# Scan preparation of a hybrid decoder step: token mixing all on one engine, key norms in another place

## The reference, cut to what matters

```python
zm = zf + (z_prev - zf) * mu_shift          # token shift, 1696 columns
r, k, v, w_lo, a_lo, g_lo = split(zm)
w_log = -softplus(-(w0 + tanh(w_lo) @ w_decay_up)) - 0.5
decay = exp(-exp(w_log))
a = sigmoid(a0 + a_lo @ w_iclr_up)
g = sigmoid(g_lo) @ w_gate_up
kk = heads(k * k_k)
kk = kk / max(sqrt(sum(kk * kk, -1)), 1e-12)    # per head of 64
k = k * (1.0 + (a - 1.0) * k_a)                 # the "key factor"
y, state = wkv_scan(r, decay, k, v, -kk, kk * a, state)
```

## Time and profile before

| what | value |
|---|---|
| time, median of 3 runs | 1613.26 us (1612.03 to 1622.89) |
| profiled execution: its time | 1620.39 us |
| profiled execution: span | 1618.7 us |
| busy: TensorE, DVE, ACT, POOL | 1256.8, 500.7, 263.7, 211.7 us |
| mean granted clock of TensorE | 0.883 |

### The profile page before, as it was taken

How to read it: one execution, slowest core, us unless ns; L and a number is a source line. 1 busy time by engine, 2 the same in 40 slices (tenths; PEclk the granted TensorE clock), 3 DMA queues, 4 the chain that set the end, 5 groups by cost and what they waited for, 6 DMA issues and landing times. The chain is left out here.

```text
span 1618.7 us, 26083 instructions
## 1 busy us (share of the span) xinstructions
PE 1256.8 (78%) x10498; PEld 775.4 (48%) x10498; DVE 500.7 (31%) x1005; ACT 263.7 (16%) x537; POOL 211.7 (13%) x247
## 2 busy tenths in 40 slices
PE   5999969989994686677455999839878788878881
PEld 3885547679992454333223774513333233323330
DVE  2002357735645452663441211241111101110113
ACT  2000233202220132453000001201111111110110
POOL 0000252100000530243311000001111101110000
PEclk9999989898997697798677999859999999998996
DMA  7022121240001853332726561259999999999964
GB/s 308 17 71 100 43 64 64 80 117 4 5 7 68 248 171 111 100 96 112 220 71 234 203 251 73 109 184 353 404 404 413 407 414 407 406 410 414 413 281 172
DMA packets 89081, 324.86 MB, mean 201 GB/s; under 512 B 25257, under 2 KB 57178, under 8 KB 74282
## 3 DMA queue, kind: packets, MB, share of 16 engines
q1 hardware_dynamic: 69018, 291.80, 46.9%
q0 software_dynamic: 11184, 25.17, 4.8%
q10 hardware_dynamic: 8768, 6.29, 1.3%
HBM read 306.36 MB, written 28.92 MB: 207 GB/s over the span
## 5 line engine op out<-in xcount | busy, mean ns | idle before, releaser
L2489 DVE TENSOR_TENSOR e_g<-e_g,PS 64x512 f32<-64x512 f32 x32 | 22.1, 690 | 332.2 <-ACT e_g L2456 332.2
L289 PE MATMUL PS<-scr,p_w 128*128 128x272 f32 (+2 forms) x448 | 105.2, 398 | 6.1 <-DVE scr L356 6.1
L2402 PE MATMUL PS<-first,e_xs 128*64 128x512 f32 x352 | 89.0, 663 | 22.5 <-DMA first<-in_w_exp_up 21.8
L894 PE MATMUL PS<-scr 128*128 128x272 f32 x384 | 92.6, 404 | 15.2 <-PEq L2559 13.2
L2402 PE MATMUL PS<-second,e_xs 128*64 128x512 f32 x352 | 84.6, 636 | 24.3 <-DMA second<-in_w_exp_up 23.6
L2402 PE MATMUL PS<-e_w,e_xs 128*64 128x512 f32 x320 | 79.7, 655 | 24.7 <-DMA e_w<-in_w_exp_up 24.6
L289 PEld LDWEIGHTS PS<-scr,p_w 128*128 128x128 f32 (+2 forms) x448 | 83.7, 187 | 27.3 <-issue 6.9
L894 PEld LDWEIGHTS PS<-scr 128*128 128x128 f32 x384 | 75.1, 197 | 31.8 <-issue 13.5
L2060 PE MATMUL PS<-m_oT,xe 128*128 128x272 f32 x256 | 64.6, 412 | 22.0 <-DMA m_oT<-scratch_ob_dram 18.2
L2345 POOL DMA_INDIRECT xe<-scratch_h_dram,toks x32 | 30.5, 954 | 386.6 <-PE PS L2392 283.8
L1193 POOL DMA_DIRECT2D c_raw<-in_cmp_pool x48 | 38.1, 796 | 264.3 <-issue 263.4
(11 more groups left out here) (545 smaller groups left out, 2011.1 us busy)
## 6 DMA issues: line engine op xcount, KB each, us to landing
first<-in_w_exp_gate SPq DMA_DIRECT2D x11, 2048.0 KB, 16.6
first<-in_w_exp_up SPq DMA_DIRECT2D x11, 2048.0 KB, 21.0
first<-in_w_exp_down SPq DMA_DIRECT2D x11, 2048.0 KB, 24.0
second<-in_w_exp_gate SPq DMA_DIRECT2D x11, 2048.0 KB, 28.4
second<-in_w_exp_up SPq DMA_DIRECT2D x11, 2048.0 KB, 32.8
second<-in_w_exp_down SPq DMA_DIRECT2D x11, 2048.0 KB, 22.9
e_w<-in_w_exp_gate SPq DMA_DIRECT2D x10, 2048.0 KB, 27.7
e_w<-in_w_exp_up SPq DMA_DIRECT2D x10, 2048.0 KB, 31.9
```

The source lines that it names most:

```text
L289: last = nc.tensor.matmul(out[:, n], w[:, s % NW, c, a:a + m], hT[:, c, n * TH:n * TH + TH], start=(c == 0), stop=(c == KC - 1))
L894: last = M(gate_ps(u)[:, n], wgate[:, u % 2, c, :], hT[:, c, n * TH:n * TH + TH], start=(c == 0), stop=(c == KC - 1))
L2402: last = M(ps, xs[:, b, c, :], w[s][m][:, c * DE:c * DE + DE], start=(c == 0), stop=(c == KC - 1))
L2489: V.tensor_tensor(g[:, b, :], g[:, b, :], psU, ALU.mult).then_inc(h_out, 1)
```

## The change

POOL no longer mixes v. It waits until `mixed` is 2, and only then clears the padding tiles. DVE mixes v as a fourth round, between k and r, with the same instructions as the other rounds; `mixed` rises after chunks 12 and 13 and after r, as before. The semaphore `v_mixed` and the waits on it on DVE and ACT are gone. The key factor's four chunks are split: chunks 0 and 1, then the four multiplications by the inverse norms, then chunks 2 and 3.

```diff
@@ gpsimd
-                pool.wait_ge(par_in, 16)
-                cs = slice(8, 12)
-                shift_rows(G_, link, cs)
-                mu = Pm("mu", 8, 4).unsqueeze(2).to_broadcast([P, 4, T])
-                link(G_.tensor_tensor(v_[:, :, 0:T], v_[:, :, 0:T], mu, ALU.mult))
-                link(G_.tensor_tensor(v_[:, :, 0:T], v_[:, :, 0:T], z[:, cs, 0:T], ALU.add))
-                pool.sem_inc(v_mixed, 1)
+                pool.wait_ge(mixed, 2)
                 link(G_.memset(v_[:, :, T:TP], 0.0))
@@ vector
-                for cs in (slice(12, 14), slice(4, 8), slice(0, 4)):
+                for cs in (slice(12, 14), slice(4, 8), slice(8, 12), slice(0, 4)):
                     shift_rows(V, link, cs)
...
-                    dve.wait_ge(mix_done, {12: 2, 4: 6, 0: 10}[cs.start])
-                    if cs.start != 4:
+                    dve.wait_ge(mix_done, {12: 2, 4: 6, 8: 10, 0: 14}[cs.start])
+                    if cs.start in (12, 0):
                         dve.sem_inc(mixed, 1)
...
-                dve.wait_ge(v_mixed, 1)
                 dve.wait_ge(lora_out, 12)
...
-                for c in range(4):
+
+                def key_factor(c):
                     link(V.tensor_scalar(BK[:, c, 1, 0:T], a_[:, c, 0:T], 1.0, Pm("k_a", c), ALU.subtract, ALU.mult))
                     link(V.scalar_tensor_tensor(out=k_[:, c, 0:T], in0=BK[:, c, 1, 0:T], scalar=1.0, in1=k_[:, c, 0:T],
                                                 op0=ALU.add, op1=ALU.mult))
+
+                for c in (0, 1):
+                    key_factor(c)
                 for c in range(4):
                     dve.wait_ge(norm_mm, c + 1)
                     link(V.tensor_tensor(kk[:, c, 0:T], kk[:, c, 0:T], wide(c % 2), ALU.mult))
                     dve.sem_inc(kk_used, 1)
+                for c in (2, 3):
+                    key_factor(c)
@@ scalar
                 act.wait_ge(mixed, 2)
-                act.wait_ge(v_mixed, 1)
```

More of the change, by code:

```diff
@@ L487, in rwkv @@
         scanned = sem("r_scanned")
-        pchain, v_mixed, mix_done = sem("r_pchain"), sem("r_v_mixed"), sem("r_mix_done")
+        pchain, mix_done = sem("r_pchain"), sem("r_mix_done")
         dchain, achain, s_init = sem("r_dchain"), sem("r_achain"), sem("r_s_init")
```

## The result

| | before | after |
|---|---|---|
| median, 20 runs each | 1617.86 us (1612.03 to 1625.52) | 1612.72 us (1607.50 to 1619.04) |
| ratio, after to before | | 0.9972, 95% interval 0.9959 to 0.9986 |
| profiled execution: time, span | 1620.39, 1618.7 us | 1610.26, 1608.6 us |
| last gate eviction, from the stage's first matmul | 118.49 us | 114.56 us |

The ratio is worth 4.5 us (2.3 to 6.6). The forecast was 8.8. Ratios leave out two executions that were far longer than the rest (1801.43 us with unit 7 between the products, 2059.48 us with 128 partitions and no gap). The last line of the table is the measure used from here on: the start of ScalarE's last gate eviction less the start of the first matmul of the stage `rwkv` (222.19 and 222.13 us).

A forecast was written before the change was run, and what follows sets the result against it. TensorE was taken to bound the changed stretch, 222 to 350 us, through its gaps and slow clock. Part 1's 1.9 plus part 2's 6.9 made 8.8 us, off the median 1613.3 to 1604.5 us; range 1600 to 1613.

The forecast's parts named there:

- Part 1, VectorE's stalls: Mixing of v: 11.3 us of VectorE stalls beside POOL go, closing TensorE's gap before the third gate unit, −1.9 us.
- first signal: `mixed` = 1 comes 3.2 us sooner, ScalarE's tanh starts at 230.3; the second comes 4.6 us sooner, near 250.3.
- Rival 3: Mixing stalls are VectorE's own, not POOL's; the added v round delays TensorE: 2.3 us slower, 1615.6 us; chance 0.03.
- Part 2, the gap: Before norm product 3: multiplications ahead of the second key factor half cut TensorE's idle from 3.96 to 0.7 us.
- Part 2, the hold on POOL: VectorE's multiplications with one PSUM operand and POOL's subtractions do not hold each other; POOL ends 1.2 us sooner.
- Part 2, the clock: Around norm product 3: full clock through the short gap; products 3 and 4 take 2.25 us, unit 7 ends at 296.8.
- stall for unit 8: TensorE waits 0.2 us for gate unit 8's weights, bounds 0 to 1.4 us.
- Rival 1: Clock still falls at the short gap before product 3: 3.8 us come back, gain 5.0 us, 1608.3 us; chance 0.14.
- The shift behind the stage: After the scan starts, barriers make the shift rigid: the last gate eviction's 8.8 us should reappear at the end.
- The absolute time: Whole kernel: 1604.5 us, the median 1613.3 less 8.8 us.
- rival 4: Whole kernel: work shifts, but scatter or a later stage swallows the gain, 1611 to 1614 us; chance 0.13.

The follow-up runs named there:

- unit 7 between the products: Changed kernel with gate unit 7 placed between norm products 2 and 3, key factor chunks 2 and 3 between multiplications 2 and 3; ratio 0.9943 to the kernel before.
- 128 partitions and no gap: Changed kernel with norm products over 128 partitions instead of 8 and only key factor chunk 0 ahead of the multiplications; ratio 0.9952 to the kernel before.
- run with wide products: Changed kernel with norm products over 128 partitions instead of 8, 1.2 us gap kept; ratios 0.9937 and, repeated, 0.9955 to the kernel before.
- two traces without a gap: Changed kernel with only key factor chunk 0 ahead of the multiplications, products over 8 partitions; ratio 0.9954 to the kernel before, last gate eviction at 112.01 and 112.19 us.
- the long gap left in place: Kernel before with only the norm products widened from 8 to 128 partitions, gap 4.16 us; ratio 0.9988, last gate eviction at 117.04 us.

## Why the prediction was wrong

The direction was right and the size was not. By its own steps:

- **Part 1, VectorE's stalls:** right. 3.3 and 8.1 us go; the first signal came at 230.19 (forecast 230.3), the second at 250.0 (250.3), the first gate eviction at 232.93 (233.0), the gap closed for 2.0 us (1.9). Rival 3, that the stalls were VectorE's own, is excluded by the 0.17 and 0.83 us.
- **Part 2, the gap:** 0.99 us where 0.7 were forecast. Relative to TensorE, VectorE's scans start 0.3 us later than in the kernel before.
- **Part 2, the hold on POOL:** right. POOL's subtractions take 1.2 us less, 6.46 and not 7.65, as worked out with no hold from the earlier trace rows; VectorE's first two multiplications take 1.59 us beside them (at 284.64), as long as in the kernel before, where POOL was done (at 289.62). The eviction that releases unit 8's weights follows. In the run with wide products, where unit 7 is fast, the evictions of units 7 and 8 are 297.26 and 304.76, 7.50 apart: a stall of 0.2 us, the forecast's figure. The Trainium skill's rule on the shared SBUF interface (GPSIMD Engine Reference, Specifications), by which VectorE instructions in a 2-port mode or with two SBUF inputs contend with POOL, agrees with these times: a multiplication here has one SBUF and one PSUM input.
- **Part 2, the clock:** this step failed. "Such a gap is shorter than the 1.93 us that left the clock at 1.00, so I count full clock". The comparison took the gap as the only cause. The 1.93 us gap lay between gate units with 128 partitions, the other one in the middle of four products with 8. In the changed kernel the clock fell 0.3 us after the second of these products had ended; in the two traces without a gap it fell while the third ran; with the products over 128 partitions and a gap of 1.2 us it did not fall. Products 3 and 4 took 4.40 us where 2.25 were forecast, and gate unit 7 took 10.06 us where 7.33 were forecast: 2.15 + 2.73 = 4.9 us of the forecast are missing. 8.8 − 4.9 = 3.9, the 3.93 us of the trace, and within the interval of the ratio, 4.5 us (2.3 to 6.6). The 0.2 us by which product 3 came late and the 0.2 us of stall for unit 8, which was not there, cancel.
- **Rival 1** is what happened to the clock, with a chance of 0.14, though not for its reason, the short gap. It was priced at the old slow spell's cost, 3.8 us, and 5.0 us of gain. It was dearer because the spell is as long as before, 10.2 us, but where 2.7 us of the old one fell into idle time, TensorE now works through nearly all of it. Of the 2.97 us taken from the gap, 2.0 had lain in the slow spell; work moved into that time ran at half speed and gave 1.0 back. That follows from the two traces; the runs with wide products show what the spell itself cost, 4.3 and 4.7 us.
- **The shift behind the stage** was taken as rigid, and the ratio agrees within its interval: 4.5 us (2.3 to 6.6) against 3.93 at the last gate eviction. A single pair of traces would have said 10.1.
- **The absolute time** says little either way. The measured 1612.72 us lies between the 1611 and 1614 of rival 4, but only because the median of three from which the forecast started was low; the ratio is clear of 1, so the gain was not swallowed by scatter.

The page "TensorE: Matmul & The Clock Gate" of the Trainium skill (Part 1) lets the clock follow how busy the engine has been. If busy means the time in which a matmul runs, the runs without a gap differ: TensorE is busy in 2.00 of 2.00 us in each window in which the clock falls. Here the measurement decides.

Left open: why matmuls over 8 partitions are followed by the fall, and why the slow spell is 3.4, 6.8, 10.2 or 13.7 us long in kernels that differ by so little. The wide products widen the weights and the streamed operand together, so which of the two counts is not shown, nor at what width between 8 and 128 the fall stops. One row bears on that: the low-rank products, over 32 partitions in pairs side by side and over 96, run for 9.5 us without a fall (window of TensorE in the changed kernel):

```profile
254.00:263.50 9.50, 9.50 (x48) 1.00 0.24 85
```

The scan's own slow spells were not studied.

## What to carry to other kernels

Before an idle gap of TensorE is blamed for a slow clock, look at the half microsecond in which the clock falls and at the matmuls ahead of it: products over a few partitions can lower it while the engine is busy. Where such a product can be padded to 128 partitions with zero weights, it costs one larger load and no time on TensorE. Here it was worth 4.3 and 4.7 us on top of the shorter gap, but only 1.45 us with the long gap left in place: the two fixes belong together. And where a slow spell stays as long as it was, idle time inside it that is filled with work gives back only half its length.

## What the runs showed of the hardware that was not expected

- Four products in a row over 8 partitions (matmuls of 512 and 32 columns) saw the clock fall to 1.2 GHz during them or just behind the first two in all seven traces, with 0 to 4.25 us of idle time; the same over 128 partitions saw no fall in two traces with 1.2 us of idle time among them and in one with none. Two such pairs over 8 partitions with a gate unit between them saw a fall after the first pair only. The 128-partition product takes as long as the 8-partition one at full clock: 1.13 and 1.12 us.
- After 128-partition products the clock held through 2.8 us of idle time and then fell, in one trace.
- A short VectorE instruction can be held until the POOL instruction beside it ends: 3.44 us for 2 elements per partition, 0.17 without POOL beside it.
